# Two mixers: attention heads weighed in pairs on column halves, with the softmax sum inverted once and applied on the way out

## What is computed

```python
s = jnp.einsum('bqhd,bkhd->bhqk', q, k) * scale      # masked: causal, or causal and dilated
w = jax.nn.softmax(s, axis=-1)
o = jnp.einsum('bhqk,bkhd->bqhd', w, v)              # per block of 128 queries
...
o = rmsnorm(o_group, group_out_norm[kind])           # over the group's 512 features
out = concat(o_lat, o_dil) @ w_out
```

## Time and profile before

| | us |
|---|---|
| median of three runs | 2954.98 (2954.85 to 2957.35) |
| the profiled execution | 2956.8 |
| its span | 2955.0 |

### The profile page before, as it was taken

The page is one execution under the profiler, slowest core; times in us unless marked ns, Lnnn a source line. Parts: engine busy times, 40 slices in busy tenths (PEclk is TensorE's granted clock), DMA queues, the critical chain, the costliest instruction groups (busy, mean ns, idle before and its releaser), DMA issues.

```text
span 2955.0 us, 42807 instructions
## 1 busy us (share of the span) xinstructions
PE 2836.9 (96%) x17352; PEld 2354.5 (80%) x17352; DVE 1554.6 (53%) x2610; ACT 1138.3 (39%) x1886; POOL 243.3 (8%) x272
## 2 busy tenths in 40 slices
PE   6999989899999999999999999999999999999998
PEld 3865889778788888878888888788888788888887
DVE  5744466454454434856644435744435865644346
ACT  4333544242242222456422224522224564422234
POOL 0000064400000000200100000000000201000001
PEclk8999999999999999999999999999999999999998
DMA  6112000022222333311223232223233301232321
GB/s 241 65 64 79 1 9 4 9 85 93 93 95 98 100 100 112 108 40 37 93 93 100 97 103 86 86 93 99 95 105 112 97 30 51 93 100 97 103 93 58
DMA packets 69779, 244.93 MB, mean 83 GB/s; under 512 B 8464, under 2 KB 10640, under 8 KB 68944
## 3 DMA queue, kind: packets, MB, share of 16 engines
q1 hardware_dynamic: 69584, 242.21, 24.9%
HBM read 234.70 MB, written 3.15 MB: 80 GB/s over the span
## 4 chain that ended last, share of the span: by engine, by line
PE 65%; DVE 5%; ACT 1%; issue 1%; POOL 0%; DVEq 0%; ACTq 0%; POOLq 0%
PE pair L247 20%; PE pair L248 19%; PE pair L249 19%; PE pair L2636 2%; PE pair L2665 2%; DVE work_at L333 1%; PE pair L2675 1%; DVE w_lo_at L190 1%; DVE residual L339 1%; DVE h_lo_at L344 1%; DVE rstd_at L529 1%; ACT w_hi_at L182 1%; PE pair L392 0%; PE pair L398 0%; PE pair L547 0%
## 5 line engine op out<-in xcount | busy, mean ns | idle before, releaser
L247 PE MATMUL pair<-h_hi_at,w_hi_at 128*128 128x512 f32 (+1 forms) x2112 | 783.5, 371 | 25.0 <-DVE h_lo_at L344 20.6
L249 PE MATMUL pair<-h_hi_at,w_lo_at 128*128 128x512 f32 (+1 forms) x2112 | 771.1, 365 | 0.0
L248 PE MATMUL pair<-h_lo_at,w_hi_at 128*128 128x512 f32 (+1 forms) x2112 | 771.0, 365 | 0.0
L182 ACT ACTIVATE w_hi_at<-w_raw 128x1024 fp32r<-128x1024 f32 x340 | 358.8, 1057 | 873.6 <-PE pair L249 862.3
L190 DVE TENSOR_TENSOR w_lo_at<-w_raw,w_hi_at 128x1024 fp32r<-128x1024 f32 x340 | 430.2, 1266 | 311.9 <-ACT w_hi_at L182 311.7
L247 PEld LDWEIGHTS pair<-h_hi_at,w_hi_at 128*128 128x128 f32 x2112 | 401.1, 190 | 106.7 <-DVE h_lo_at L344 29.2
L248 PEld LDWEIGHTS pair<-h_lo_at,w_hi_at 128*128 128x128 f32 x2112 | 401.7, 190 | 62.6 <-issue 0.5
L249 PEld LDWEIGHTS pair<-h_hi_at,w_lo_at 128*128 128x128 f32 x2112 | 401.4, 190 | 62.4
L2390 DVE TENSOR_TENSOR work_at<-pair,rstd_at 128x512 f32<-128x512 f32 x176 | 121.3, 691 | 350.5 <-PE pair L249 350.4
L247 PE MATMUL pair<-a_hi_at,w_hi_at 128*128 128x512 f32 (+1 forms) x792 | 290.4, 367 | 0.0
L248 PE MATMUL pair<-a_lo_at,w_hi_at 128*128 128x512 f32 (+1 forms) x792 | 289.7, 366 | 0.0
(11 more groups left out here) (439 smaller groups left out, 3886.2 us busy)
## 6 DMA issues: line engine op xcount, KB each, us to landing
w_raw<-in_weights SPq DMA_DIRECT2D x431, 512.0 KB, 3.5
residual<-in_x SPq DMA_DIRECT2D x1, 2048.0 KB, 11.3
cos_sin_at<-rope_table SPq DMA_DIRECT2D x2, 1024.0 KB, 4.8
by_sin_at<-delta_at SPq DMA_DIRECT2D x32, 64.0 KB, 2.0
by_sin_at<-kd_at SPq DMA_DIRECT2D x32, 64.0 KB, 2.0
out<-residual SPq DMA_DIRECT2D x16, 128.0 KB, 1.7
q_wide<-in_ctx SPq DMA_DIRECT2D x1, 1024.0 KB, 12.9
rope_table<-zb SPq DMA_DIRECT2D x1, 1024.0 KB, 4.2
```

Source lines behind the costliest of these rows:

```text
L182: eng.activation(self.w_hi[:, g % self.split].rearrange("p k n -> p (k n)"), self.w_raw[:, slot], ACT.Copy).then_inc(self.w_hi_ready, 1)
L247: pe.matmul(out, sh, mh, start=start, stop=False)
L248: pe.matmul(out, sh, ml, start=False, stop=False)
L249: return pe.matmul(out, sl, mh, start=False, stop=stop)
```

## The change

- The items go by pairs of heads: for each pair the blocks 3, 2, 0, 1, and for each block both heads. Four items (two blocks, two heads) are a **unit**; a kind has 8.
- weigh(j) takes a pair of items. Now v (64 columns) is the stationary side and probs_t (128 columns) streams; the output is [64 features, 128 tokens], head 0 on partitions 0 to 63 and head 1 on 64 to 127 of one bank. So o comes out as [features, tokens], and the transposes of features are gone.
- The ones column and its memsets are gone. exp also accumulates the sum of its row. For each unit VectorE inverts four columns of sums (invert), TensorE spreads them over 64 rows by a product of the broadcast inverse with the identity (share), ScalarE copies that to SBUF (copy_share), and VectorE multiplies the weighed values by it as it stores them (store), 256 columns at once.
- Squares are taken unit by unit (16 of 256 columns), POOL adds them, and TensorE sums them (sums, 16 records of one column) and spreads the inverse root (spread, 8 records of 128 columns) into a bank, by which scale multiplies.

```diff
-        order = [(h, n) for pair in ((3, 0), (2, 1)) for h in range(8) for n in pair]
-        self.items = [(kind, h, n) for kind in range(2) for h, n in order]
+        self.items = [(kind, 2 * pair + h, n) for kind in range(2) for pair in range(4) for n in (3, 2, 0, 1) for h in range(2)]
...
-        def weigh(i):
+        def weigh(j):
+            u, (bank, _, kind, part) = j // 2, self.unit(j // 2)
+            n = self.items[2 * j][2]
+            at = n * P - part * HALF
+            pe.wait_ge(*self.copied(2 * j + 2))
+            if j % 2 == 0 and u >= 2:
+                pe.wait_ge(*self.stored(u - 1))
...
             for c in range(w // P):
-                last = pe.matmul(kit.banks[6 + i % 2][:, 0:HD + 1], b["probs_t"][:, i % 3, c * P:(c + 1) * P], v[:, c, head], start=(c == 0),
-                                 stop=(c == w // P - 1))
+                for h in range(2):
+                    last = pe.matmul(bank[h * HD:(h + 1) * HD, at:at + P], v[:, c, head + h],
+                                     b["probs_t"][:, (2 * j + h) % 3, c * P:(c + 1) * P], start=(c == 0), stop=(c == w // P - 1),
+                                     skip_group_check=True)
...
+        def share(u):
+            bank, _, _, part = self.unit(u)
+            pe.wait_ge(*self.inverted(u + 1))
+            for j in range(2):
+                at = HALF + self.items[4 * u + 2 * j][2] * P - part * HALF
+                for h in range(2):
+                    column = u % 2 * 4 + 2 * j + h
+                    last = pe.matmul(bank[h * HD:(h + 1) * HD, at:at + P], b["inv"][:, column:column + 1].to_broadcast([P, HD]),
+                                     ident, start=True, stop=True, skip_group_check=True)
...
+        def sums(kind):
+            for c in range(4):
+                tok = slice(c * P, (c + 1) * P)
+                pe.matmul(bank[:, c:c + 1], b["total"][:, tok], one, start=True, stop=False)
+                last = pe.matmul(bank[:, c:c + 1], b["unit_sq"][:, 1 - c // 2, c % 2 * P:(c % 2 + 1) * P], one, start=False, stop=True)
...
+        def spread(kind):
+            for c in range(4):
+                last = pe.matmul(kit.banks[self.SPREAD_BANK[kind]][:, c * P:(c + 1) * P],
+                                 b["m_inv"][:, at:at + 1].to_broadcast([P, P]), ident, start=True, stop=True)
...
-        for i in range(self.ITEMS + 4):
+        for i in range(self.ITEMS + 3):
             if i < self.ITEMS:
                 score(i)
...
             if i < 32:
                 values(i)
-            if i >= 4:
-                weigh(i - 4)
-            if i in self.TURN_AT:
...
-                features(m, 0)
+            if i >= 4 and i % 2 == 0:
+                weigh((i - 4) // 2)
+            if i >= 6 and i % 4 == 2:
+                share((i - 6) // 4)
+            if i == self.ROOT_AT - 1:
+                sums(0)
+            if i == self.ROOT_AT + 5:
+                spread(0)
             if i == self.ITEMS + 1:
                 first_features(0)
...
+        first_features(2)
+        sums(1)
+        first_features(3)
+        spread(1)
         first_features(1)
-        for f in range(4):
-            features(4 + f, 4 + f)
...
-        def square(kind, c):
-            act.activation(b["group_sq"][:, :], b[("o_lat", "o_dil")[kind]][:, c], ACT.Square,
-                           accum_out=b["m_total"][:, 4 * kind + c:4 * kind + c + 1]).then_inc(self.m_squared.sem, 1)
+        def copy_share(u):
+            act.activation(b["unit_share"][:, u % 2], self.unit(u)[0][:, HALF:], ACT.Copy).then_inc(self.share_copied.sem, 1)
+        def square(u):
+            act.activation(self.unit_square(u), self.unit(u)[1], ACT.Square).then_inc(self.m_squared.sem, 1)
...
+            if i >= 7 and i % 4 == 3:
+                copy_share((i - 7) // 4)
+            if i >= 9 and i % 4 == 1:
+                square((i - 9) // 4)
...
-            dve.reciprocal(inv, weighed[:, HD:HD + 1]).then_inc(self.inverted.sem, 1)
-            dve.tensor_scalar(out, weighed[:, 0:HD], inv, None, ALU.mult).then_inc(self.stored.sem, 1)
+        def invert(u):
+            dve.wait_ge(*self.exped(4 * u + 4))
+            dve.reciprocal(b["inv"][:, at], b["share"][:, at]).then_inc(self.inverted.sem, 1)
+        def store(u):
+            dve.wait_ge(*self.share_copied(u + 1))
+            dve.wait_ge(*self.weighed(2 * u + 2))
+            dve.tensor_tensor(out, bank[:, 0:HALF], b["unit_share"][:, u % 2], ALU.mult).then_inc(self.stored.sem, 1)
...
+        def scale(m):
+            dve.scalar_tensor_tensor(o, o, group(m), kit.banks[self.SPREAD_BANK[kind]][:, :], ALU.mult, ALU.mult).then_inc(
+                self.m_scaled.sem, 1)
...
+        store(self.UNITS - 1)
         inverse(1)
+        for f in range(5):
+            if f < 4:
+                scale(4 + f)
+            if f:
+                rest_m(3 + f)
```

More of the change, by code:

```diff
@@ L2523, in item, with unit, unit_square @@
         if kind == 0:
-            return b["qh"][0:96, h, tok], b["kh"][0:96, h, 0:w], b["vm"], b["o_lat"][:, n, h * HD:(h + 1) * HD], w, h
-        return self.kit.delta[:, h, tok], b["kd"][:, h // 2, 0:w], b["vd"], b["o_dil"][:, n, h * HD:(h + 1) * HD], w, h
+            return b["qh"][0:96, h, tok], b["kh"][0:96, h, 0:w], b["vm"], w, h
+        return self.kit.delta[:, h, tok], b["kd"][:, h // 2, 0:w], b["vd"], w, h
+    def unit(self, u):
+        kind, pair, part = u // 8, u // 2 % 4, 1 - u % 2
+        return self.kit.banks[6 + u % 2], self.b[("o_lat", "o_dil")[kind]][:, pair, cols(part)], kind, part
+    def unit_square(self, u):
+        return self.b["total"][:, cols(1 - u % 2)] if u % 8 < 2 else self.b["unit_sq"][:, u % 2]
     def sp(self, sp):
@@ L2560, in pool @@
                 pool.wait_ge(*self.q_cleared(2 * r))
+        for kind in range(2):
+            for u in range(8 * kind + 2, 8 * kind + 6):
+                total = b["total"][:, cols(1 - u % 2)]
+                pool.wait_ge(*self.m_squared(u + 1))
+                if u % 8 >= 4:
+                    pool.wait_ge(*self.m_added(4 * kind + u % 8 - 3))
+                pool.tensor_tensor(total, total, self.unit_square(u), ALU.add).then_inc(self.m_added.sem, 1)
         self.exit.pool(pool)
@@ L2621, in score @@
             kind, head, _ = self.items[i]
-            q, k, _, _, w, _ = self.item(i)
+            q, k, _, w, _ = self.item(i)
             if i >= 2:
@@ L2790, in exp @@
         def exp(i):
-            w = self.item(i)[4]
+            w = self.item(i)[3]
             act.wait_ge(*self.masked(i + 1))
@@ L2811, in root @@
[L2811 removed]
+            act.wait_ge(*self.m_summed(kind + 1))
+            act.activation(b["m_root"][:, 4 * kind:4 * kind + 4], kit.banks[self.SPREAD_BANK[kind]][:, 0:4], ACT.Sqrt,
                            scale=1.0 / 512, bias=kit.eps[:, 0:1]).then_inc(self.m_rooted.sem, 1)
[L2814 to L2816 removed]
@@ L2818, in act, with round_m @@
-        done = 0
-        for i in range(self.ITEMS + 2):
-            if i >= 2:
-                copy(i - 2)
+        def round_m(m):
+            act.wait_ge(*self.m_scaled(m + 1))
+            act.activation(hi[:, m], b[("o_lat", "o_dil")[m // 4]][:, m % 4], ACT.Copy).then_inc(self.m_rounded.sem, 1)
+        for i in range(self.ITEMS + 3):
+            if self.TURN_BEHIND <= i < self.ITEMS + self.TURN_BEHIND:
+                copy(i - self.TURN_BEHIND)
             if i < self.ITEMS:
@@ L3307, in program @@
             b = layer_buffers(kit)
-            for name, width in (("peak", 4), ("inv", 4), ("by_token", 4), ("m_total", 8), ("m_root", 8), ("m_inv", 8)):
+            for name, width in (("peak", 4), ("share", 8), ("inv", 8), ("by_token", 4), ("m_root", 8), ("m_inv", 8)):
                 b[name] = layers.enter_context(nc.sbuf_tensor(name, [P, width], F32))
```

176 lines of the change are left out of this document (83 added, 93 removed).

## The result

| | before | after |
|---|---|---|
| median (12 runs each) | 2956.26 us (2954.53 to 2961.39) | 2964.67 us (2960.27 to 2967.86) |
| ratio after to before | | 1.0025, interval 1.0016 to 1.0034 |
| span of the profiled execution | 2955.0 | 2962.4 |

The account below looks back on a forecast made before the run. TensorE's own stream was taken to bind the mixers. Terms -16.0 + 10.2 + 7.0 + 0.8 + 1.0 + 1.5 + 0.3 + 1.5 = 6.3 us a mixer, +12.6 on 2955.0: 2967.5 us, range 2950 to 2982.

Parts of the forecast that it names:

- Weighing, -16.0, full overlap: Each mixer's weighing: both column halves run at once, 17.6 us in place of 33.6, so -16.0 us.
- Rival D: At weighing and shares, the halves don't overlap: 24 us a mixer more, 3015 us; chance 0.08.
- A visit at 0.32: Each switch into and out of the weighing's tiled layout costs 0.32 us; 32 a mixer, +10.2 us.
- Rival C: At each of 32 weighings a visit costs nothing where the next weights are ready: faster, 2947 us; chance 0.12.
- Shares, 0.44 each: In each of a mixer's 16 units, four products of inv against the identity take 0.44 us: +7.0 us.
- Kind 0, 68 to 70 in the text: Expected sign in the trace: kind 0 of a mixer should take 68 to 70 us.
- +0.3 for the start: Start of kind 0: larger first exps stand ahead of w_make_hi, on which TensorE's values wait: +0.3 us a mixer.
- Waits for the copy in kind 1, 0.35 and 0.23: In each eight items of kind 1, weighing waits 0.35 and 0.23 us for a copy: +1.5 us a mixer.
- ScalarE in items 32 to 39, +1.0: Kind 1 items with eight half tiles: ScalarE takes longer than TensorE, +1.0 us a mixer, bounds 0 and 1.5.
- Behind the items, +1.5: Behind a mixer's items: sum, spread and VectorE's two operations for each k take 3.9 us, +1.5 us.
- Rival A: Kind 1: ScalarE and the copy before each weighing bind, 4.8 us a mixer more, 2977 us; chance 0.20.
- Rival B: No change: waits fall under the drains and the tail is no longer, 2.0 us a mixer, 2959 us; chance 0.18.

Follow-up runs that it names:

- the later weighing: Kernel after with merged kind 0 visits, fourth buffer, VectorE root steps, two output tiles, earlier drain, and kind 1 pairs weighed one item later: 2950.22 us, ratio 0.9969.

## Why the prediction held, and where it was off

The forecast was 2967.5 with slower at 0.70; measured is 2964.67, slower, 3 under the forecast. Its sum was +12.6 on a median of three runs that lay 1.3 under the one of twelve; the medians are 8.4 apart. The two mixers are 5.0 + 6.5 = **11.5 us** longer. The span grew by 7.4 only: the stretch between the mixers is 2.9 shorter, the part ahead of them 1.0 and the part behind 0.2, where the change has no instruction. For the 2.9 the granted clock is the cause that the rows show; so a part of this case's difference is where the falls of the clock happened to stand. The part ahead, the same instructions in all twelve traces, takes from 1261.4 to 1271.6 us: that is as wide as most differences here, so a single span says little, and the comparisons above go by stages and by medians.

By its own steps:

- **Weighing, -16.0, full overlap.** Right in the overlap: a pair of records every 0.109. Rival D is out. The rule on row groups that it took from the Trainium skill's page "TensorE: Matmul & The Clock Gate", Part 3 (a weight load overlaps products in flight only when its row group differs) doesn't hold here: both halves use all 128 rows, and their weight loads start 0.007 apart, as their products do. What the step got wrong is the old price: it took 0.105 for every record, the rate of the eight of the earlier trace rows, where batches of two, four and six take 0.17, 0.39 and 0.61 in all, 32.1 us a mixer and not 33.6.
- **A visit at 0.32.** Nearly: 0.36 by one batch, 0.34 as two experiments have it. Rival C is out. What the step left out is that a weighing before had a price on its way out too: behind the eight records of the earlier trace rows the score's second record comes 0.165 later, where 0.107 is work. Some 0.057 at each of 64 weighings is 3.7 us that went. By these starts weighings, visits and shares cost 4.5 us for each eight items of kind 0 before and after, 35.8 a mixer at that rate in both, where the sum had +1.2.
- **Shares, 0.44 each.** Right: four pairs, 0.109 apart.
- **Kind 0, 68 to 70 in the text.** The terms gave +0.9 on the 64.1 between the scores; measured -0.2. Eight items take 16.55 before and after, which is 0.6 of the 1.1; the rest lies in the first eight, 14.32 in place of 14.48, where the sum had +0.3 for the start. The 68 to 70 came from the rounder cut of the earlier trace rows, on which -0.2 is 67.8.
- **Waits for the copy in kind 1, 0.35 and 0.23.** Right: 0.30 and 0.20 to 0.27 in each eight items.
- **ScalarE in items 32 to 39, +1.0.** 0.79 where 0.27 is usual: 0.5, within its bounds.
- **Behind the items, +1.5.** Right to 0.1. Inside it, 0.9 were lost at k = 5 and 6 in place of 1.3.
- **The step that failed: what was not in the sum.** It took the other waits of kind 1 as unchanged and never said so. Kind 0's root with its table loads grew from 1.12 to 2.37 (0.5 of it since the new order puts larger blocks around it), and the wait for the last drain of values from 1.02 to 1.50: +1.7 a mixer. With them the terms would give 16.1 where the mixers, the clock's part left out, took 10.0 more. Of the 3.0 a mixer between, 1.2 are the weighings, 0.5 the start of kind 0, 0.5 ScalarE's term, and 0.8, in kind 1, wasn't traced to an item. So the total came near in part by luck: two errors of opposite sign, 1.7 and 3.0 a mixer.
- **The clock in mixer 2, +1.5.** Not foreseen by any term.
- **Rival A** (ScalarE binds at each weighing, 2977): kind 1 has its signs (ScalarE is busy 45.0 of 53.7 us, and a visit there is nearly free), but the waits at the weighings are 1.9 a mixer, within the 2.5 that the sum had for them and not 4.8 more. **Rival B** (2959): the tail is longer, as was said against it.

## What to carry to other kernels

Two products on two column halves ran at once here, but going in and out cost 0.34 us each time where TensorE binds, so small products of one layout belong into one batch; with 4 to 20 records, the batches here were too small to gain. Where another engine binds, the same visit is nearly free and merging gains nothing: price each edit in the stage where it falls. When the order of the work changes, look again at every wait that was there before, the ones that nothing in the diff names too.

## What was not expected of the hardware

- Products on the two column halves don't only overlap as neighbours: with eight records of one half ahead, those of the other began, as the starts are read here, 0.005 us behind the fifth.
- After the same 23.9 us with 19.66 of TensorE's busy time in both mixers of the changed kernel, the granted clock stayed at 1.00 in mixer 1 (1352.9 to 1358.3) and was 0.68 in mixer 2, which is a part of the stretch at 1.2 GHz: 1.5 us.
- The falls of the granted clock stood in the same places in the two traces of one kernel, and in others in kernels that differ only far ahead of them: 0, 1.4 or 2.9 us in a stretch of the same instructions. What decides it wasn't found. A difference of 0.1% here can be no more than that; with the later weighing the same stretch has 2.9 against it and the kernel is still the fastest.
